# Last expert of a layer in pieces, 1/rms of the mixer applied at the evictions, and x moved in two parts

## The chip, the cores and the metric

One core of a Trainium2 chip runs the whole program. The metric is the device time of one execution in microseconds; lower is better. Engines: PE (TensorE), DVE (VectorE), ACT (ScalarE), POOL (GpSimd), and SP (SyncE), which here issues every DMA.

## What is computed

Two layers on x, 256 tokens by 1,024 features, float32. In each layer:

```python
u = rms_norm(x, norm_mix_g[l]) @ w_in[l]          # 1024 -> 3328 columns
aq, ak, av, bq, bf, bi, bg, cb, cc, cx = split(u)
o_a = differential_attention(aq, ak, av, ...)     # 4 heads, RMS norm of q and k
o_b = hgrn2(bq, bf, bi, bg, ...)                  # gated recurrence, chunks of 64
h = cc * cx; y = conv_w[0] * shift2(h) + conv_w[1] * shift1(h) + conv_w[2] * h
o_c = cb * y
x = x + concat(o_a, o_b, o_c) @ w_out[l]
h = rms_norm(x, norm_ffn_g[l])
# top-1 of 4 groups, top-2 of its 8 experts; expert = (silu(h Wg) * (h Wu)) Wd, 1024 -> 512 -> 1024
x = x + sum over the two chosen experts of gate * expert(h)
```

`rms_norm` divides each row (token) by the root of its mean square plus 1e-6 and multiplies by a gain per feature. The division commutes with the projection: it can be applied to the rows of u.

## The kernel before, in words

Tokens lie in two tiles of 128 rows (`TI` = 2). Five engine programs run side by side and meet at semaphores; each engine's order is written out by hand. A `Signal` counts, and `after(l, n)` is the value that its n-th event of layer l reaches.

**Start of a layer (mixer_norm, L1213).** ACT squares the rows of x and sums them (L899), DVE makes 1/rms by three Newton steps (`rsqrt`, L1182 to L1200), scales x by it into `h` (`normed`, L1204), PE transposes 128x128 blocks of `h` (L579), and DVE evicts them times the gain into `hT` (`take_transposed`, L1210). In layer 0 DVE first makes the rotary angles from the positions (`rotations`, L1095), and x arrives in one DMA (L371).

**Mixer.** PE multiplies `hT` with the sections of w_in as they land in the ring: `project_columns` (L649) gives features on partitions (HGRN's q and forget gate, and the three convolution parts), `project_rows` (L642) gives tokens on partitions. Thirteen results are evicted by ACT (`copy_out`, L901 to L905). The HGRN levels and the attention run between the projections. POOL does the output gate and the convolution (L491 to L512): gate + 1 (L499), gate product (L502), `ccT * cxT` (L504); then ACT multiplies by the taps (L1019), and POOL adds the two shifted parts (L508) and multiplies by `cbT` (L510), which signals `conv_ok`. PE waits for that (L811) before the first part of the output projection (L712), after transposing the attention output that DVE finishes (L791, L1401). After the taps, ACT has the squares for HGRN's norm (L1023).

**Experts.** 32 experts, 8 turns (`GROUPS`) of 4 units (`UG`), one expert each with 32 slots (`CAP`). A turn gathers its tokens by a one-hot product (L588), and transposes the gate matrix (L593). Each unit has "up" (L605: gate and up matrices side by side, moving width 256, four column groups of 32), silu and product and a 32x32 block transpose (L1155 to L1163), and "down" (L620), whose four 32-row results are copied to rows 32i to 32i+31 of `ye` by ACT (L890) and DVE (L1168). At the end of the turn four matmuls with 512 columns scatter all four units back to tokens (L628), and four DVE adds put them on x (L1173). A unit's three matrices are 2 MB each and live in a ring; SP issues gate and up of unit i when up of unit i-2 is done, and down when down of unit i-2 is done (L407 to L414), so two units are in flight:

```python
e.wait_ge(S.gu_ps.sem, S.gu_ps.after(turn, i - 1))
part(full, sg, ex, 0)
part(full, su, ex, 1)
e.wait_ge(S.ye_ps.sem, S.ye_ps.after(turn, i - 1))
part(full, sd, ex, 2)
```

(the semaphore starts at 2, so this waits for unit i-2). At the end of a layer the next layer's first sections of w_in queue behind the last unit's matrices (L417 to L429). At the end of the program SP stores x in one DMA (L485).

## Time and profile before

| | |
|---|---|
| median of 3 runs | 1287.55 us (1287.08 to 1288.71) |
| the profiled execution, its own time | 1283.46 us |
| its span, first to last instruction | 1281.7 us |
| mean granted TensorE clock | 0.864 |
| PE busy | 892.9 us (70%) |
| DVE busy | 522.3 us (41%) |
| ACT, POOL busy | 166.4 us, 25.9 us |
| moved by DMA | 442.05 MB, 345 GB/s over the span |

Layer 0's mixer runs to about 180 us, its experts to 642, layer 1's mixer to about 815, and its experts to the end. Busy shares are averages over stages with different limits, so each stage is to be read by itself. A float32 matmul stands in the profile as two records, a transpose as one. A granted clock of 1.00 is 2.4 GHz, 0.50 is 1.2 GHz.

### The profile page before, as it was taken

The numbers are of one execution on the slowest core, as the hardware profiler recorded it, in microseconds if no ns is written. First come the engines' busy times: TensorE is split into PE (matmuls) and PEld (weight loads), VectorE is DVE, ScalarE is ACT, GpSimd is POOL, SyncE is SP. The second block draws the span as 40 slices with busy tenths as digits, with TensorE's granted clock in tenths as the row PEclk, the third lists the DMA queues.
The fourth block names the chain that finished last, engine by engine and source line by source line (L and its number), as shares of the span: only waits on it lengthen the run. The fifth ranks groups of instructions, "written<-read, shape, count | busy, mean of one in ns | idle before, by whom it ended". The sixth has DMA issues, their size and how long they took to land.

```text
span 1281.7 us, 19451 instructions
## 1 busy us (share of the span) xinstructions
PE 892.9 (70%) x8069; PEld 531.1 (41%) x8069; DVE 522.3 (41%) x1309; ACT 166.4 (13%) x480; POOL 25.9 (2%) x63
## 2 busy tenths in 40 slices
PE   5999775766666566746679989757666575657665
PEld 4558453434334233424254574534333242324242
DVE  6666462423323232323257563624333232413232
ACT  2324110100000000000013241000000000000000
POOL 2001100000000000000000020000000000000000
PEclk9999877978888887888779999778788787978788
DMA  7824548799999999999984253498999999999995
GB/s 257 330 99 167 227 164 358 320 428 429 428 429 428 428 428 429 428 428 424 411 291 165 84 202 146 177 393 356 429 427 429 428 430 428 427 429 430 427 423 233
DMA packets 53986, 442.05 MB, mean 345 GB/s; under 512 B 9120, under 2 KB 12208, under 8 KB 29104
## 3 DMA queue, kind: packets, MB, share of 16 engines
q1 hardware_dynamic: 53936, 441.36, 83.3%
q8 instruction: 34, 0.56, 0.2%
...
## 4 chain that ended last, share of the span: by engine, by line
PE 54%; DMA 27%; DVE 14%; issue 3%; ACT 2%; SPq 0%; DVEq 0%; ACTq 0%
DMA ring<-in_expert_w_up 27%; PE bank L605 16%; PE bank L645 9%; PE bank L620 6%; PE bank L588 5%; PE bank L654 5%; PE bank L628 5%; PE bank L712 4%; DVE work L1157 2%; DVE work L1168 1%; PE bank L676 1%; DVE work L1163 1%; PE bank L579 1%; DVE work L1159 1%; DVE work L1161 1%
## 5 line engine op out<-in xcount | busy, mean ns | idle before, releaser
L605 PE MATMUL bank<-ring,work 128*32 128x256 f32 x4096 | 280.7, 435 | 118.6 <-DMA ring<-in_expert_w_up 118.2
L620 PE MATMUL bank<-ring,work 128*32 128x256 f32 x1856 | 154.7, 490 | 153.1 <-DVE work L1163 153.1
L605 PEld LDWEIGHTS bank<-ring,work 128*32 128x32 f32 x4096 | 153.2, 125 | 245.3 <-issue 158.7
L620 PEld LDWEIGHTS bank<-ring,work 128*32 128x32 f32 x1856 | 68.0, 135 | 231.0 <-DVE work L1163 180.1
L1155 DVE TENSOR_SCALAR work<-work 128x128 f32<-128x128 f32 x64 | 14.5, 227 | 359.0 <-ACT work L886 359.0
L1168 DVE COPY work<-bank 32x256 f32<-32x256 f32 x128 | 54.3, 424 | 162.9 <-PE bank L620 161.9
L645 PE MATMUL bank<-ring,hT 128*128 128x512 f32 x256 | 112.4, 593 | 0.0
L588 PE MATMUL bank<-work,h 128*128 128x128 f32 x512 | 78.4, 325 | 41.5 <-DVE work L1135 36.5
L588 PEld LDWEIGHTS bank<-work,h 128*128 128x128 f32 x512 | 75.4, 238 | 53.3 <-DVE work L1135 47.6
L890 ACT ACTIVATE work<-bank 32x256 f32<-32x256 f32 x128 | 47.8, 374 | 304.1 <-PE bank L620 303.3
L654 PE MATMUL bank<-hT,ring 128*128 128x256 f32 x320 | 75.5, 398 | 0.8 <-DVE hT L1210 0.8
L628 PE MATMUL bank<-work 128*128 128x512 f32 x128 | 58.7, 602 | 17.3 <-DVE work L1168 17.3
L645 PEld LDWEIGHTS bank<-ring,hT 128*128 128x128 f32 x256 | 47.7, 190 | 54.9 <-issue 54.5
L654 PEld LDWEIGHTS bank<-hT,ring 128*128 128x128 f32 x320 | 63.5, 201 | 10.7 <-DVE hT L1210 1.2
L886 ACT ACTIVATE work<-bank 128x128 f32<-128x128 f32 x64 | 17.8, 278 | 353.9 <-PE bank L605 353.9
L1157 DVE RECIPROCAL work<-work 128x128 f32<-128x128 f32 x64 | 61.0, 953 | 2.2
L712 PE MATMUL bank<-ring,hT 128*128 128x512 f32 x128 | 58.2, 611 | 2.8 <-ACT hT L1035 2.8
L1173 DVE TENSOR_TENSOR x<-bank,x 128x512 f32<-128x512 f32 x64 | 44.3, 692 | 28.5 <-PE bank L628 28.5
L628 PEld LDWEIGHTS bank<-work 128*128 128x128 f32 x128 | 23.0, 189 | 48.5 <-issue 48.5
L1148 DVE TENSOR_TENSOR work<-bank,gffn 128x512 f32<-128x512 f32 x32 | 21.9, 691 | 45.9 <-PE bank L588 45.9
L712 PEld LDWEIGHTS bank<-ring,hT 128*128 128x128 f32 x128 | 24.9, 198 | 32.1 <-issue 32.1
L905 ACT ACTIVATE work<-bank 128x512 f32<-128x512 f32 x26 | 15.5, 596 | 123.5 <-PE bank L645 71.5
(256 smaller groups left out, 655.0 us busy)
## 6 DMA issues: line engine op xcount, KB each, us to landing
...
maps<-in_expert_w_down SPq DMA_DIRECT2D x2, 2048.0 KB, 12.7
...
ring<-in_w_in SPq DMA_DIRECT2D x2, 1024.0 KB, 5.4
```

Of the source, the lines that this page charges most:

```text
L588: last = T.matmul(bank[half][:, k * P:k * P + P], h[:, i, 4 * half + k, :], sel[:, i, :], start=(i == 0), stop=(i == TI - 1))
L605: last = T.matmul(bank[GU_BANK[i % 2]][CAP * j:CAP * j + CAP, 0:2 * P], xg[:, k, CAP * i:CAP * i + CAP], gate_up[:, :, k, P * j:P * j + P] ...
L620: last = T.matmul(bank[5][CAP * q:CAP * q + CAP, 0:2 * P], actT[i % 2][:, CAP * j:CAP * j + CAP], down[j][:, 2 * P * q:2 * P * q + 2 * P], ...
L628: T.matmul(bank[(6, 7, 0, 1)[n]][:, :], gatT[:, i * P:i * P + P], ye[:, half * 512:half * 512 + 512], start=True, stop=True).then_inc(S.sc ...
L645: last = T.matmul(bank[b][:, :], hT[:, k, i * P:i * P + P], W[:, k, :], start=(k == 0), stop=(k == KT - 1))
L654: last = T.matmul(bank[b][:, c * SEQ:c * SEQ + SEQ], W[:, k, c0:c0 + P], hT[:, k, :], start=(k == 0), stop=(k == KT - 1))
L712: last = T.matmul(bank[2 * i + half][:, :], mixT[:, k, i * P:i * P + P], W[:, k, :], start=(k == 6), stop=(k == 3))
L890: last = A(ye[CAP * i:CAP * i + CAP, 2 * P * q:2 * P * q + 2 * P], bank[5][CAP * q:CAP * q + CAP, 0:2 * P], ACT.Copy)
L1148: TT(xg[:, 4 * half:4 * half + 4, :], bank[half][:, :].rearrange("p (k c) -> p k c", k=4), gffn[:, l, 4 * half:4 * half + 4].unsqueeze(2). ...
L1157: V.reciprocal(r, r).then_inc(c.step(), 1)
L1168: last = V.tensor_copy(ye[CAP * i:CAP * i + CAP, 2 * P * q:2 * P * q + 2 * P], bank[5][CAP * q:CAP * q + CAP, 0:2 * P])
L1173: TT(xs, bank[(6, 7, 0, 1)[n]][:, :], xs, ALU.add).then_inc(S.x_added.sem, 1)
```

## The change

- x is loaded in two DMAs, one for each 128 tokens, ahead of the gains and the positions, and stored in two.
- PE transposes x itself; 1/rms is made beside the projections. It is applied at the evictions: as ACT's scale where tokens are on partitions; for columns, PE spreads it over a row (`ones` times a diagonal, two matmuls of width 128), ACT copies that row, DVE multiplies HGRN's two parts by it while evicting (`take_columns`), and POOL multiplies `cbT` once and `ccT` twice.
- The last turn of a layer takes its last unit in pieces: gate alone, then the scatter of the first three units (96 rows), then up in two halves of 1 MB, then down in two halves. The four 32-row results stay on their partitions (one ACT and one DVE copy of 64x256), and eight matmuls of 32 rows by 256 columns scatter them into 8 banks, with the gate matrix of the last unit repeated four times (`spread`). DVE adds each tile of 128 tokens in one operation, and the next layer (or the store) starts on each tile by itself.

The core of the diff (`+` and `-` as usual):

```diff
+        rstd_row = sb("rstd_row", [P, SEQ])
+        diag = hg[:, Q_, 0:TI * P].rearrange("p (i t) -> p i t", i=TI)
...
+            rows_of = [a["x"][0][i * P:i * P + P] for i in range(TI)]
+            e.dma_start(x[:, 0, :], rows_of[0]).then_inc(x_in[0].sem, 16)
+            e.dma_start(x[:, 1, :], rows_of[1]).then_inc(x_in[1].sem, 16)
+            e.dma_start(gmix[:, :, :], by_feature("norm_mix_g")).then_inc(gain_in.sem, 16)
             e.dma_start(pos_i[:, :], a["positions"][0].rearrange("(i p) -> p i", p=P),
                         allow_slow_non_contiguous=True).then_inc(pos_in.sem, 16)
-            e.dma_start(gmix[:, :, :], by_feature("norm_mix_g")).then_inc(gain_in.sem, 16)
-            e.dma_start(x[:, :, :], a["x"][0].rearrange("(i p) d -> p i d", p=P)).then_inc(x_in.sem, 16)
             mixer_section(0, 0)
...
+                last = l * GROUPS + GROUPS - 1
+                for i in range(UG - 1):
+                    unit(ring_full, main, last, i, (GROUPS - 1) * UG + i)
+                sg, su, sd = slots_of(UG - 1)
+                e.wait_ge(main.gu_ps.sem, main.gu_ps.after(last, UG - 2))
+                part(ring_full, sg, NE - 1, 0)
+                w_up = a["expert_w_up"][l:l + 1, NE - 1:NE].rearrange("l e (p k) n -> p (l e k n)", k=KT)
+                for half in range(2):
+                    c = slice(half * SLOT // 2, half * SLOT // 2 + SLOT // 2)
+                    e.dma_start(slot(su)[:, c], w_up[:, c]).then_inc(up_half[half].sem, 16)
+                e.wait_ge(main.ye_ps.sem, main.ye_ps.after(last, UG - 2))
+                w_down = a["expert_w_down"][l:l + 1, NE - 1:NE].rearrange("l e (p j) n -> p (l e j n)", p=P)
+                for half in range(2):
+                    c = slice(half * SLOT // 2, half * SLOT // 2 + SLOT // 2)
+                    e.dma_start(slot(sd)[:, c], w_down[:, c]).then_inc(down_half[half].sem, 16)
+            for i in range(TI):
+                stream_ready(e, DEPTH, i)
+                e.dma_start(out[0][i * P:i * P + P], x[:, i, :]).then_inc(out_done.sem, 16)
+            e.wait_ge(out_done.sem, 16 * TI)
...
+                e.wait_ge(row_sb.sem, row_sb.after(l, 1))
                 settle(e)
                 G.tensor_scalar(egate, egate, 1.0, None, ALU.add).then_inc(gate_sum.sem, 1)
...
+                by_token = rstd_row[:, :].unsqueeze(1).to_broadcast([P, 2, SEQ])
+                for n, t in enumerate((cbT, ccT)):
+                    v = t.rearrange("p (c t) -> p c t", c=2)
+                    e.wait_ge(proj_sb.sem, proj_sb.after(l, 9 + n))
+                    G.tensor_tensor(v, v, by_token, ALU.mult).then_inc(conv_scaled.sem, 1)
+                e.wait_ge(conv_scaled.sem, conv_scaled.after(l, 2))
+                v = ccT.rearrange("p (c t) -> p c t", c=2)
+                G.tensor_tensor(v, v, by_token, ALU.mult).then_inc(conv_scaled.sem, 1)
+                e.wait_ge(proj_sb.sem, proj_sb.after(l, 11))
+                e.wait_ge(conv_scaled.sem, conv_scaled.after(l, 3))
                 G.tensor_tensor(ccT, ccT, cxT, ALU.mult).then_inc(conv_in.sem, 1)
                 e.wait_ge(taps_ok.sem, taps_ok.after(l, 1))
...
+            def last_experts(l, turn, loaded):
+
+                S = main
+                gathered(S, turn, True)
+                expert_units(S, turn, IN_TURN[0:2 * (UG - 1)], slots_of, loaded)
+                i = UG - 1
+                sg, su, sd = slots_of(i)
+                W = [slot(n).rearrange("p (k n) -> p k n", k=KT) for n in (sg, su)]
+
+                def half_up(part, ks):
+
+                    for k in ks:
+                        for j in range(4):
+                            last = T.matmul(bank[LAST_GU[part]][CAP * j:CAP * j + CAP, 0:P],
+                                            xg[:, k, CAP * i:CAP * i + CAP], W[part][:, k, P * j:P * j + P],
+                                            start=(k == 0), stop=(k == KT - 1))
+                    return last
+
+                e.wait_ge(ring_full[sg].sem, loaded(sg, i))
+                half_up(0, range(KT)).then_inc(gate_ps.sem, 1)
+
+                e.wait_ge(S.gat_sb.sem, S.gat_sb.after(turn, 1))
+                e.wait_ge(S.ye_act.sem, S.ye_act.after(turn, UG - 1))
+                e.wait_ge(S.ye_dve.sem, S.ye_dve.after(turn, UG - 1))
+                early = CAP * (UG - 1)
+                for n in range(4):
+                    T.matmul(bank[n][:, :], gatT[0:early, n // 2 * P:n // 2 * P + P], ye[0:early, n % 2 * 512:n % 2 * 512 + 512],
+                             start=True, stop=True).then_inc(S.scat_ps.sem, 1)
+
+                e.wait_ge(up_half[0].sem, up_half[0].after(l, 16))
+                half_up(1, range(0, 4))
+                e.wait_ge(up_half[1].sem, up_half[1].after(l, 16))
+                half_up(1, range(4, KT)).then_inc(S.gu_ps.sem, 1)
+                e.wait_ge(S.act_ok.sem, S.act_ok.after(turn, UG))
+                down = down_tiles(sd)
+                for j in range(4):
+                    if j % 2 == 0:
+                        e.wait_ge(down_half[j // 2].sem, down_half[j // 2].after(l, 16))
+                    for q in range(4):
+                        last = T.matmul(bank[5][CAP * q:CAP * q + CAP, 0:2 * P], actT[i % 2][:, CAP * j:CAP * j + CAP],
+                                        down[j][:, 2 * P * q:2 * P * q + 2 * P], start=(j == 0), stop=(j == 3))
+                last.then_inc(S.ye_ps.sem, 1)
+
+                e.wait_ge(S.x_added.sem, S.x_added.after(turn, 4))
+                e.wait_ge(S.ye_act.sem, S.ye_act.after(turn, UG))
+                e.wait_ge(S.ye_dve.sem, S.ye_dve.after(turn, UG))
+                for t in range(TI):
+                    for q in range(4):
+                        rows = slice(CAP * q, CAP * q + CAP)
+                        last = T.matmul(bank[4 * t + q][:, 0:2 * P], spreadT[rows, t * P:t * P + P], ye_last[rows, :],
+                                        start=True, stop=True)
+                    last.then_inc(tail_ps.sem, 1)
...
-                    e.wait_ge(h_ok.sem, h_ok.after(l, i + 1))
-                    transposed_rows(i, h[:, i, :, :])
+                    stream_ready(e, l, i)
+                    transposed_rows(i, x[:, i, :].rearrange("p (c k) -> p k c", k=KT))
...
                 W = section(0)
                 project_columns(W, 4, 0)
+                e.wait_ge(rstd_ok.sem, rstd_ok.after(l, 1))
+                for i in range(TI):
+                    last = T.matmul(bank[3][:, i * P:i * P + P], ones[:, :], diag[:, i, :], start=True, stop=True)
+                last.then_inc(row_ps.sem, 1)
                 project_columns(W, 5, 1)
...
-                    A(u[:, n - 1, :], bank[b][:, :], ACT.Copy).then_inc(proj_sb.sem, 1)
+                    if n <= 10:
+                        A(u[:, n - 1, :], bank[b][:, :], ACT.Copy, scale=rstd[:, (n - 1) % TI:(n - 1) % TI + 1]).then_inc(proj_sb.sem, 1)
+                    else:
+                        A(u[:, n - 1, :], bank[b][:, :], ACT.Copy).then_inc(proj_sb.sem, 1)
...
+                e.wait_ge(row_ps.sem, row_ps.after(l, 1))
+                A(rstd_row[:, :], bank[3][:, 0:SEQ], ACT.Copy).then_inc(row_sb.sem, 1)
+                e.wait_ge(cols_sb.sem, cols_sb.after(l, 1))
                 A(hg[:, Z0_, :], bq, ACT.Exp, scale=-1.0).then_inc(hg_act.sem, 1)
-                copy_out(2)
...
+            def last_experts(l, turn):
+                S, i, c = main, UG - 1, Chain(last_dve, l)
+                e.wait_ge(main.dve.sem, main.dve.after(l * (GROUPS - 1) + GROUPS - 2, DVE_G))
+                gathered(S, turn, codes, l, c, None, True)
+                expert_units(S, turn, IN_TURN[0:2 * (UG - 1)], c)
+                (gate, up), r = (bank[b][:, 0:P] for b in LAST_GU), silr[i % 2]
+                e.wait_ge(S.gu_exp.sem, S.gu_exp.after(turn, UG))
+                TS(r, sil[i % 2], 1.0, None, ALU.add).then_inc(c.step(), 1)
+                e.wait_ge(c.sem, c.last())
+                V.reciprocal(r, r).then_inc(c.step(), 1)
+                e.wait_ge(c.sem, c.last())
+                TT(r, gate, r, ALU.mult).then_inc(c.step(), 1)
+                for n in range(4):
+                    e.wait_ge(S.scat_ps.sem, S.scat_ps.after(turn, n + 1))
+                    xs = x[:, n // 2, n % 2 * 512:n % 2 * 512 + 512]
+                    TT(xs, bank[n][:, :], xs, ALU.add).then_inc(S.x_added.sem, 1)
+                e.wait_ge(S.gu_ps.sem, S.gu_ps.after(turn, UG))
+                e.wait_ge(c.sem, c.last())
+                TT(actv[i % 2], up, r, ALU.mult).then_inc(c.step(), 1)
+                e.wait_ge(c.sem, c.last())
+                V.transpose(actT[i % 2].rearrange("p (j c) -> p j c", j=4),
+                            actv[i % 2].rearrange("p (r j) -> p j r", j=4)).then_inc(S.act_ok.sem, 1)
+                e.wait_ge(S.ye_ps.sem, S.ye_ps.after(turn, UG))
+                V.tensor_copy(ye_last[P // 2:P, :], bank[5][P // 2:P, 0:2 * P]).then_inc(S.ye_dve.sem, 1)
+                e.wait_ge(S.x_added.sem, S.x_added.after(turn, 4))
+                for t in range(TI):
+                    e.wait_ge(tail_ps.sem, tail_ps.after(l, t + 1))
+                    xs = x[:, t, :].rearrange("p (q n) -> p q n", q=4)
+                    TT(xs, psum[:, 4 * t:4 * t + 4, 0:2 * P], xs, ALU.add).then_inc(tail_added.sem, 1)
+                c.end()
+
...
+                if spread_too:
+                    TT(gat, gat, gtmp, ALU.add).then_inc(c.step(), 1)
+                    e.wait_ge(c.sem, c.last())
+                    for i in range(TI):
+                        last = V.tensor_copy(spread[:, i, :].rearrange("p (q s) -> p q s", q=4),
+                                             gat[:, i, CAP * (UG - 1):CAP * UG].unsqueeze(1).to_broadcast([P, 4, CAP]))
+                        last.then_inc(S.gat_ok.sem if i else c.step(), 1)
...
                 def mixer_norm():
-                    e.wait_ge(sums_ok.sem, sums_ok.after(l, 2))
-                    rsqrt(rstd, ssq, D)
-                    for i in range(TI):
-                        normed(i).then_inc(h_ok.sem, 1)
                     if l == 0:
                         e.wait_ge(gain_in.sem, 16)
                     for n in range(4):
                         take_transposed(n, gmix)
+                    e.wait_ge(sums_ok.sem, sums_ok.after(l, 2))
+                    rsqrt(rstd, ssq, D)
+                    for i in range(TI):
+                        last = TS(diag[:, i, :], ident[:, :], rstd[:, i:i + 1], None, ALU.mult)
+                        last.then_inc(rstd_ok.sem if i else c.step(), 1)
                     V.memset(sT, 0.0).then_inc(c.step(), 1)
+
+                def take_columns(n, dst):
+
+                    e.wait_ge(proj_ps.sem, proj_ps.after(l, n))
+                    TT(dst.rearrange("p (c t) -> p c t", c=2), bank[3 + n][:, :].rearrange("p (c t) -> p c t", c=2),
+                       rstd_row[:, :].unsqueeze(1).to_broadcast([P, 2, SEQ]), ALU.mult).then_inc(cols_sb.sem, 1)
...
```

## Rows read from the trace of the kernel before

**Rows 1.** The page: GB/s moved, in 40 equal slices of the span.
```profile
GB/s 257 330 99 167 227 164 358 320 428 429 428 429 428 428 428 429 428 428 424 411 291 165 84 202 146 177 393 356 429 427 429 428 430 428 427 429 430 427 423 233
```

**Rows 2.** Chain of waits in order of time: start, us, what.
```profile
114.44 2.02 PE bank L703 x16
...
626.79 5.38 PE bank L605 x64
...
634.86 1.98 PE bank L620 x32
...
637.87 3.69 PE bank L628 x8
...
641.58 0.70 DVE x L1173
...
652.56 16.52 PE bank L654 x64
```

**Rows 3.** Instructions in order of time, layer 1's last turn: start, us, engine, line.
```profile
1232.88 0.33 SPq L397 DMA_DIRECT2D ring<-in_expert_w_gate  x1
...
1247.22 5.73 PE L605 MATMUL bank<-ring,work 128*32 128x256 f32 x64 [0.78 <-DMA ring<-in_expert_w_up]
...
1255.67 1.45 PEld L620 LDWEIGHTS bank<-ring,work 128*32 128x32 f32 x32 [3.21 <-DVE work L1163]
1255.68 1.93 PE L620 MATMUL bank<-ring,work 128*32 128x256 f32 x32 [2.73 <-DVE work L1163]
...
1261.90 5.22 PE L605 MATMUL bank<-ring,work 128*32 128x256 f32 x64 [4.29 <-DMA ring<-in_expert_w_up]
...
1277.30 0.40 SPq L485 DMA_DIRECT2D out<-x  x1
```

**Rows 4.** The same view, start of the program.
```profile
1.78 0.47 SPq L371 DMA_DIRECT2D x<-in_x  x1
...
3.00 1.27 DVE L1100 CAST small<-pos_i 128x2 f32<-128x2 int32 x1 [3.00 <-DMA pos_i<-in_positions]
...
12.19 2.21 DVE L1204 TENSOR_SCALAR h<-x,small 128x1024 f32<-128x1024 f32 x2
...
18.12 16.31 PE L654 MATMUL bank<-hT,ring 128*128 128x256 f32 x64
```

**Rows 5.** PE by stretches: us, PE busy (records), granted clock, DMA share, GB/s.
```profile
616.20:626.70 10.50, 2.78 (x36) 0.68 1.00 424
...
652.50:656.00 3.50, 3.44 (x8) 0.50 1.04 385
...
1247.00:1253.00 6.00, 5.73 (x64) 0.63 0.99 421
```

**Rows 6.** Groups by line and form: count, busy us, mean ns, idle before.
```profile
L1163 DVE STREAM_TRANSPOSE work<-work 128x128 f32<-128x128 f32 x64 | 25.8, 404 | 2.2
...
L1346 DVE TENSOR_TENSOR work<-work,small 128x1024 f32<-128x1024 f32 x4 | 4.9, 1226 | 0.1
```

**Rows 7.** DMA issues: count, KB each, median us to landing.
```profile
x<-in_x SPq DMA_DIRECT2D x1, 1024.0 KB, 5.3
out<-x SPq DMA_DIRECT2D x1, 1024.0 KB, 4.0
```

**Rows 8.** Instructions in order of time, end of layer 0's mixer: POOL, DVE, PE.
```profile
124.66 1.26 POOL L504 TENSOR_TENSOR work<-work 128x512 f32<-128x512 f32 x1
124.76 3.31 DVE L1386 TENSOR_TENSOR maps<-maps,small 128x2048 f32<-128x2048 f32 x1
...
128.54 3.16 POOL L508 TENSOR_TENSOR work<-work 128x510 f32<-128x510 f32 x2 [2.62 <-ACT work L1019]
...
129.33 1.24 DVE L1185 TENSOR_SCALAR small<-small 128x4 f32<-128x4 f32 x1
...
131.78 1.27 POOL L510 TENSOR_TENSOR hT<-work 128x512 f32<-128x512 f32 x1
...
136.87 4.52 PE L712 MATMUL bank<-ring,hT 128*128 128x512 f32 x8
```

132 lines of the change are left out of this document (82 added, 50 removed).

## Prediction

> **What bounds the kernel now.** I read the page's strips first: in both expert stages the DMA moves 428 to 430 GB/s in nearly every slice, slice after slice, and falls away in the two mixer stages [rows 1]. So the expert stages run at the pace of the weights, and the mixers at that of the engines. A change to either end of an expert stage therefore shifts all that follows; one inside it is hidden. The chain of waits in order of time gives the seam between the layers [rows 2]: the last up matrix lands at 626.79, and from there to 652.56, where the mixer's first projection starts, it is a pure chain of short steps, 25.8 us. The instructions in order of time give the same tail at the end of the program [rows 3]: up lands at 1261.90, the store is issued at 1277.30 and takes 4.0 us [rows 7], so 19.4 us. The last down matrix is behind up in one stream. At 429 GB/s 2 MB take 4.9 us, so gate has landed 4.9 us before up (622 and 1257), the first half of up 2.4 us before, and down 4.9 us after it (631.7, 1266.8). These are the places that the change touches, with the start of the program and the mixer's evictions.
>
> **The sum, part by part** (negative is a gain), in the profiled execution's times.
>
> Start of the program. The DVE begins its rotations at 3.00, when the positions land, and has them and the rsqrt done for the scaling at 12.19; the projection starts at 18.12 [rows 4]. Of this the change removes rsqrt, scaling and the transposes' wait for them from the path. It also puts both parts of x ahead of the positions on SP. The whole x lands 5.3 us after its issue at 1.78 [rows 4, 7]; issued some 1 us earlier, with positions behind it, the positions land at 6.0 to 6.3 instead of 3.0. Rotations took 6.3 us (3.00 to 9.3), partly beside POOL's set-up; I take 5.5. Then four takes at 0.7 us: 6.1 + 5.5 + 2.8 = 14.5, so **-3.5**. Bounds: positions at 4.3 give -4.5, rotations at full 6.3 us and positions at 7 give -2.0.
>
> Tail of each layer. New order on PE: gate alone after down of unit 2; scatter of the first 96 slots; two halves of up; down; the row-tiled scatter. Gate or up alone is 64 records of width 128. The full 64 records of width 256 take 3.6 to 5.4 us; the trace has no narrow ones. Below: half the stream, 1.8 us. Above: no gain, 3.6 us. Weight loads of 32 columns have been issued at 1.45 us for 32, 45 ns each [rows 3], which gives 2.9 us; it is the nearest row and I take it. The new scatter is the old one, 3.67 us, but earlier.
> - End of the program: down of unit 2 ends at 1257.6 [rows 3], gate to 1260.6, scatter to 1264.3, up to 1267.2 (both halves are there), multiply and transpose 0.75 (0.40 of it the transpose [rows 6]), down 1.98 to 1269.95 (landed at 1266.8 latest), the copies 0.55 (one of 64x256 each instead of two of 32x256), so 1270.5. A group of four 32-row matmuls: the nearest row is the scores' (L703), 64 rows high, eight matmuls of width 256 (16 records) in 2.02 us [rows 2], so 1.0 for four; bounds 0.45 and 1.7. Then two adds of 1,024 columns, 1.23 us each by the row of that width [rows 6]: 1271.5, 1272.75, 1274.0. Half the store: 4.0 us [rows 7] less 1.2 us of bytes at 429 GB/s = 2.8. End at 1276.9 instead of 1281.3: **-4.4**. Bounds -6.8 (narrow at 1.8 us; then down's landing is the limit) and -0.7 (narrow at 3.6 us and row tiles serial).
> - Seam: the granted clock was 0.68 between 616.2 and 626.7 [rows 5], so gate from 622.0 is half at the low level: 4.4 us, to 626.4; scatter to 630.1, up to 633.0, down from 633.75 to 635.7, copies to 636.3, matmuls 1.0, adds to 638.55 and 639.8. The old last add ended at 642.3. Then transposes of x directly (the first half beside the second add), and four takes on DVE, 0.69 us each, from 639.85: projection at 642.7 instead of 652.56, **-9.9**. The squares, rsqrt and the two diagonals (2.3 + 2.3 + 0.3 us) run beside the first 8 us of projection. Bounds: -13.7 and -6.8.
>
> For the row tiles I used 1.0 us for a group of four. The Trainium skill, TensorEngine Tiling (Array Packing), section Tiling Modes, has four tiles of 32 rows that work independently, which would be one stream, 0.45 us by this trace's rate; the sum would be 0.5 us lower per layer, and no row here shows such tiles.
>
> More issues on SP (one more for up, one for down, one for the store and for x, at 0.33 to 0.47 us each) stand behind nothing: SP's queue is ahead of the stream. The last group's two extra copies on DVE and two transposes on PE (up to 0.4 us) delay the issue for unit 2, but the stream still has some 3 us in hand there (unit 2's gate and up, issued from 1232.88, have landed at 1247.22 [rows 3], 14.3 us for 9.8 us of bytes and some 1 to 2 us of latency): 0, bound +0.8 in all. If that cover is gone, all of it counts.
>
> Mixer, PE: two matmuls of width 128 for the row of 1/rms, 0.45 us each layer on the path since PE is busy throughout the projections: **+0.9**. Evictions: the scale rides on copies that exist. Two move from ACT (0.60) to DVE (0.69) and wait for the row's copy, 1 us later for the HGRN chain, which ran over 5 us ahead of PE's need: 0.
>
> Mixer, POOL: three new products of 128x512 stand between the gate product and the old conv product, ahead of the taps (ACT) and ahead of the three last POOL steps, on which PE's first part of the output projection waits. One takes 1.26 us [rows 8]. The rows show more: POOL and DVE shut each other out. DVE's 2,048-wide product takes 3.31 us where two of 1,024 make 2.45, and starts beside a POOL product; the first POOL add waits for the DVE product (3.16 us for two that need 2.2); and DVE steps of 4 elements take 1.24 us while POOL adds [rows 8]. So I lay both queues out in turn: products at 124.7, 128.1, 130.5, 131.9 with DVE's two between them; taps (2.6 us) 133.2 to 135.8; POOL's last three until 140.2 instead of 133.05. PE had been ready for it at 136.87, so the cover of 3.8 us is overrun by **3.3** per layer, **+6.6**. ACT's taps stand ahead of the squares for the HGRN norm, whose result comes at 143.7, before PE's 144.5: no further loss. Bounds per layer: 0 (only 3.8 us of products, exactly the cover) and +5.5 (PE falls to the low clock in the longer gap).
>
> Sum: -3.5 - 9.9 - 4.4 + 0.9 + 6.6 = **-10.3** against the profiled execution (1283.46; span 1281.7), 1273.2. The median of the runs is 1287.55, 4.1 above it; I take the difference over: 1277.3.
>
> **Rivals.**
> 1. The POOL products are hidden. For: the cover of 3.8 us equals three products. Against: the mutual exclusion just read [rows 8]. Then -16.9: 1270.7. Chance 0.18.
> 2. PE stays at the high clock over the seam. The projection of layer 1 begins at 0.50 [rows 5] after some 6 us without PE work but transposes; the new gaps are under 2 us. Against: the unit that started at 1247.22 after gaps of that kind ran at 0.63 [rows 3, 5]. Then -2.7 more: 1274.6. Chance 0.12.
> 3. Narrow matmuls cost as much as full ones and the row tiles run one after another: the seam gains only 6.8 and the end only 0.7: -3.5 - 6.8 - 0.7 + 7.5 = -3.5, 1284.0. Chance 0.12, half of it within the bound of no change.
> 4. Slower: the POOL products are the mechanism. They sit ahead of the taps in POOL's queue; gains without them are 16.9 us, so from 8.5 us of delay per layer the change loses, that is when the three take (8.5 + 3.8)/3 = 4.1 us each, against 1.26 to 2.0 seen. At 5.5 us each the delay is 12.7 per layer: -16.9 + 25.4 = +8.5, 1296. Chance 0.04.
> 5. It does less than it says: the halves of up and down land no earlier than the whole (the sixteen engines skewed). PE is behind the stream there, so it costs under 1 us; inside the forecast.
>
> **How the numbers follow.** Forecast and its near misses 0.54, rivals 0.18, 0.12, 0.12, 0.04. A measurement of this kernel tells 0.2% (2.6 us) from no change. Faster: 0.54 + 0.18 + 0.12 + 0.06, less 0.04 for several upper bounds together = 0.86; within 0.2%: 0.10; slower 0.04. The range reaches from rival 1 with a part of the seam's bound (1268) to rival 3 (1284).
>
> **What the profile after would show.** Projection in layer 0 from about 14.5; first projection of layer 1 10 us after the last up half, with the same low clock at its start; POOL products of 1.26 to 2 us in line behind the gate product and PE's first output projection waiting on the last of them, not on DVE; a store of 2.8 us. I am wrong if the narrow records are not near 45 ns, if that wait ends elsewhere, or if the expert stages, which I left as they are, get longer or shorter.

## The result, and the profile after

The changed kernel takes 1274.78 us (median of 9 runs, 1270.47 to 1280.96) where the kernel before, run beside it, takes 1288.71 (9 runs, 1281.24 to 1296.96): a ratio of 0.9881, 95% interval 0.9846 to 0.9917. The forecast was 1277.3. The profiled execution of the changed kernel took 1270.47 us with a span of 1268.7, that of before 1283.46 and 1281.7, so the sum stands beside a difference of 13.0 us. Both profiled executions lie 4 to 5 us below their medians, the changed kernel's is the lowest of its nine, so the two differences, 13.0 and 13.9, agree.

The page after: the strips of GB/s and of the granted clock.
```profile
PEclk9999788879888888888899989778888888879789
GB/s 258 355 84 194 200 166 320 291 428 429 429 429 428 428 428 428 429 429 424 420 389 195 100 245 87 184 390 330 429 428 428 428 429 429 429 428 428 428 423 316
```
The two plateaus at some 428 GB/s stand as in [rows 1], but the slices just ahead of the first one changed: 320 and 291 where there were 358 and 320. The first two turns of the expert stage are not yet at the pace of the weights.

The start of the program after (start us, us, engine, line).
```profile
2.15 0.47 SPq L389 DMA_DIRECT2D pos_i<-in_positions  x1
...
5.04 3.65 PE L622 MATMUL psum<-ident,x 128*128 128x128 f32 x16 [5.04 <-POOL masks L594]
...
6.96 0.21 DVE L1229 CAST small<-pos_i 128x2 f32<-128x2 int32 x1 [6.96 <-DMA pos_i<-in_positions]
...
12.01 2.48 DVE L1384 TENSOR_TENSOR hT<-psum,gmix 128x512 f32<-128x512 f32 x4
...
14.75 1.65 PE L761 MATMUL psum<-hT,ring 128*128 128x256 f32 x3
```
Against [rows 4] the scaling of h is gone and the transposes run at 5.04 beside the rest; the positions now land at 6.96, and VectorE's rotations and takes behind them set the start, 14.75 for 18.12.

The seam between the layers after, PE and what it waits for, in order of time.
```profile
625.21 1.92 PE L655 MATMUL psum<-ring,work 128*32 128x128 f32 x64
...
627.06 3.70 PE L668 MATMUL psum<-work 96*128 96x512 f32 x8
...
630.69 1.95 PE L655 MATMUL psum<-ring,work 128*32 128x128 f32 x64
...
633.50 1.07 PE L681 MATMUL psum<-ring,work 128*32 128x256 f32 x16 [0.85 <-DVE work L1286]
...
635.10 1.07 PE L681 MATMUL psum<-ring,work 128*32 128x256 f32 x16 [0.53 <-DMA ring<-in_expert_w_down]
...
636.81 1.15 PE L691 MATMUL psum<-work 32*128 32x256 f32 x16 [0.64 <-DVE work L1289]
637.65 2.35 DVE L1294 TENSOR_TENSOR x<-psum,x 128x1024 f32<-128x1024 f32 x2 [0.99 <-PE psum L691]
...
642.45 7.17 PE L761 MATMUL psum<-hT,ring 128*128 128x256 f32 x32 [1.23 <-DVE hT L1384]
```
From the last up matrix's matmuls to the projection it is 11.8 us (630.69 to 642.45) where [rows 2] have 25.8. Gate alone takes 1.92, the scatter of the first 96 slots stands ahead of up, up takes 1.95, and then PE waits for the second half of down: the stream, not PE, ends this chain. The projection's first 32 records take 7.17 us.

PE by stretches after: us, PE busy, PEld, DVE, ACT, POOL, granted clock, DMA share, GB/s.
```profile
642.45:651.45 9.00, 9.00 (x44) 7.99 (x45) 4.57 (x20) 0.59 (x2) 0.00 (x0) 1.00 1.05 386
```
Where [rows 5] have the low level (0.50, that is 1.2 GHz) the clock is now at its high level, 2.4 GHz, from the first column on.

The end of the program after, in order of time, and two rows of the DMA issues.
```profile
1255.62 1.95 PE L655 MATMUL psum<-ring,work 128*32 128x128 f32 x64
...
1260.56 1.07 PE L681 MATMUL psum<-ring,work 128*32 128x256 f32 x16 [1.06 <-DMA ring<-in_expert_w_down]
...
1262.27 1.15 PE L691 MATMUL psum<-work 32*128 32x256 f32 x16 [0.64 <-DVE work L1289]
...
1264.36 1.47 SPq L518 DMA_DIRECT2D out<-x  x2
```
```profile
x<-in_x SPq DMA_DIRECT2D x2, 512.0 KB, 4.5
out<-x SPq DMA_DIRECT2D x2, 512.0 KB, 2.7
```
13.1 us from up to the end of the span, 19.8 in [rows 3]; the half store lands in 2.7 us, the whole one took 4.0 [rows 7].

The end of layer 0's mixer after, POOL with DVE and ACT beside it.
```profile
119.66 1.27 POOL L536 TENSOR_TENSOR work<-work 128x512 f32<-128x512 f32 x1 [22.29 <-DVE work L1632]
...
120.89 4.54 POOL L541 TENSOR_TENSOR work<-work,rstd_row 128x512 f32<-128x512 f32 x2
120.99 3.31 DVE L1570 TENSOR_TENSOR maps<-maps,small 128x2048 f32<-128x2048 f32 x1
...
125.51 2.13 POOL L544 TENSOR_TENSOR work<-work,rstd_row 128x512 f32<-128x512 f32 x1
126.43 1.23 DVE L1359 TENSOR_SCALAR small<-small 128x4 f32<-128x4 f32 x1
...
127.79 1.27 POOL L547 TENSOR_TENSOR work<-work 128x512 f32<-128x512 f32 x1
...
129.10 2.50 ACT L1148 ACTIVATE work<-work,table 128x256 f32<-128x256 f32 x6 [6.87 <-POOL work L547]
...
131.67 2.75 POOL L551 TENSOR_TENSOR work<-work 128x510 f32<-128x510 f32 x2 [2.61 <-ACT work L1148]
```
Three new products (L541 twice, L544) take 6.7 us where three undisturbed ones would take 3.8, and all that follows on POOL stands behind them [rows 8]. PE's own rows show what the first output projection waits for:
```profile
135.93 5.91 PE L822 MATMUL psum<-ring,hT 128*128 128x512 f32 x8 [2.65 <-POOL hT L553]
```
L553 is POOL's last step. The eight records take 5.91 us where they took 4.52 [rows 8].

### The profile page after: what moved, and what is told of

Same layout as the page of the kernel before. It is cut to its first block, busy times and chain, and to the rows that moved or that the text cites. A ratio compares the mean times of both kernels' runs of the same rounds, so it can differ in the third digit from the quotient of the medians.

```text
span 1268.7 us, 19814 instructions
## 1 busy us (share of the span) xinstructions
PE 888.4 (70%) x8241; PEld 530.9 (42%) x8241; DVE 526.1 (41%) x1319; ACT 165.1 (13%) x476; POOL 38.5 (3%) x69
## 4 chain that ended last, share of the span: by engine, by line
PE 53%; DMA 28%; DVE 11%; issue 3%; POOL 2%; ACT 1%; SPq 1%; DVEq 0%; POOLq 0%
DMA ring<-in_expert_w_up 24%; PE psum L719 15%; PE psum L752 9%; PE psum L631 6%; PE psum L734 6%; PE psum L822 5%; PE psum L761 5%; PE psum L704 4%; DMA ring<-in_expert_w_down 3%; DVE work L1336 2%; PE psum L786 1%; DVE work L1342 1%; DVE work L1347 1%; DVE work L1338 1%; DVE work L1340 1%
## 5 line engine op out<-in xcount | busy, mean ns | idle before, releaser
L719 PE MATMUL psum<-ring,work 128*32 128x256 f32 x3968 | 270.4, 433 | 114.4 <-DMA ring<-in_expert_w_up 114.4
L734 PE MATMUL psum<-ring,work 128*32 128x256 f32 x1792 | 147.2, 485 | 147.6 <-DVE work L1342 147.6
L719 PEld LDWEIGHTS psum<-ring,work 128*32 128x32 f32 x3968 | 147.7, 125 | 236.0 <-issue 148.0
L734 PEld LDWEIGHTS psum<-ring,work 128*32 128x32 f32 x1792 | 64.6, 133 | 221.1 <-DVE work L1342 173.6
L1347 DVE COPY work<-psum 32x256 f32<-32x256 f32 x124 | 52.6, 424 | 155.2 <-PE psum L734 154.2
L752 PE MATMUL psum<-ring,hT 128*128 128x512 f32 x256 | 112.4, 593 | 0.0
L631 PE MATMUL psum<-work,h 128*128 128x128 f32 x512 | 79.6, 328 | 43.2 <-DVE work L1304 36.2
L631 PEld LDWEIGHTS psum<-work,h 128*128 128x128 f32 x512 | 76.3, 240 | 55.4 <-DVE work L1304 47.2
L761 PE MATMUL psum<-hT,ring 128*128 128x256 f32 x320 | 72.5, 385 | 1.2 <-DVE hT L1384 1.2
L752 PEld LDWEIGHTS psum<-ring,hT 128*128 128x128 f32 x256 | 47.7, 190 | 54.9 <-issue 54.5
L822 PE MATMUL psum<-ring,hT 128*128 128x512 f32 x128 | 60.0, 627 | 8.1 <-POOL hT L553 5.3
L761 PEld LDWEIGHTS psum<-hT,ring 128*128 128x128 f32 x320 | 61.0, 193 | 9.8 <-DVE hT L1384 1.4
L704 PE MATMUL psum<-work 128*128 128x512 f32 x112 | 51.4, 601 | 15.2 <-DVE work L1347 15.2
L822 PEld LDWEIGHTS psum<-ring,hT 128*128 128x128 f32 x128 | 25.3, 202 | 39.2 <-issue 39.2
## 6 DMA issues: line engine op xcount, KB each, us to landing
maps<-in_expert_w_down SPq DMA_DIRECT2D x2, 2048.0 KB, 12.2
```

Source lines behind the costliest of these rows:

```text
L631: last = T.matmul(bank[half][:, k * P:k * P + P], h[:, i, 4 * half + k, :], sel[:, i, :], start=(i == 0), stop=(i == TI - 1))
L704: T.matmul(bank[(6, 7, 0, 1)[n]][:, :], gatT[:, i * P:i * P + P], ye[:, half * 512:half * 512 + 512], start=True, stop=True).then_inc(S.sc ...
L719: last = T.matmul(bank[GU_BANK[i % 2]][CAP * j:CAP * j + CAP, 0:2 * P], xg[:, k, CAP * i:CAP * i + CAP], gate_up[:, :, k, P * j:P * j + P] ...
L734: last = T.matmul(bank[5][CAP * q:CAP * q + CAP, 0:2 * P], actT[i % 2][:, CAP * j:CAP * j + CAP], down[j][:, 2 * P * q:2 * P * q + 2 * P], ...
L752: last = T.matmul(bank[b][:, :], hT[:, k, i * P:i * P + P], W[:, k, :], start=(k == 0), stop=(k == KT - 1))
L761: last = T.matmul(bank[b][:, c * SEQ:c * SEQ + SEQ], W[:, k, c0:c0 + P], hT[:, k, :], start=(k == 0), stop=(k == KT - 1))
```

## The experiments

All of them are read by one division of the span, worked out from the starts of PE's rows in the profiled executions: start of the projection, of the scores' second group, of the first output projection, of the gather in the first and in the last turn of the expert stage. The columns are the us between them; "seam" reaches from the last turn's gather in layer 0 to the projection of layer 1, "end" from the last gather to the end. A gather is not tied to one place of the weight stream, so a few us can move between neighbouring columns of the expert stage; where that matters, the count below goes from a landing.

Ratios are to the kernel before, run beside each group. Its medians were 1294.96 us (e1 to e4), 1291.83 (e5 to e8) and 1288.78 (e9 to e11), with single runs from 1281 to 1297, so kernels of different groups are compared by stretches first.

| kernel | to proj. | to scores | to out | to gather 0 | 7 turns | seam | to scores | to out | to gather 0 | 7 turns | end | span |
|---|---|---|---|---|---|---|---|---|---|---|---|---|
| before | 18.12 | 96.32 | 22.43 | 49.29 | 401.90 | 64.50 | 96.53 | 22.43 | 49.40 | 402.62 | 58.16 | 1281.7 |
| changed | 14.75 | 95.91 | 25.27 | 50.67 | 404.22 | 51.63 | 94.54 | 25.27 | 49.83 | 402.07 | 54.54 | 1268.7 |
| e5 (again) | 14.76 | 96.32 | 25.27 | 50.89 | 403.64 | 52.27 | 94.54 | 25.28 | 49.91 | 402.09 | 54.63 | 1269.6 |
| e1 tail undone | 14.75 | 96.56 | 25.22 | 51.04 | 403.96 | 60.16 | 94.54 | 25.26 | 51.00 | 403.42 | 61.19 | 1287.1 |
| e2 norm undone | 21.56 | 94.09 | 22.44 | 49.44 | 401.97 | 59.21 | 95.82 | 22.44 | 50.73 | 402.97 | 55.73 | 1276.4 |
| e3 no products | 14.79 | 96.65 | 22.43 | 50.71 | 403.34 | 52.54 | 94.54 | 22.44 | 49.54 | 401.93 | 54.59 | 1263.5 |
| e4 POOL early | 14.76 | 96.72 | 22.43 | 50.74 | 403.55 | 52.39 | 94.53 | 22.43 | 49.54 | 402.40 | 54.71 | 1264.2 |
| e6 no row tiles | 14.78 | 97.27 | 25.22 | 51.40 | 404.42 | 55.69 | 94.54 | 25.22 | 51.49 | 404.56 | 56.01 | 1280.6 |
| e7 pieces only | 14.78 | 96.04 | 25.23 | 50.77 | 403.43 | 56.89 | 94.54 | 25.24 | 51.05 | 403.55 | 58.18 | 1279.7 |
| e8 positions early | 13.12 | 96.29 | 22.44 | 50.50 | 403.18 | 53.16 | 94.54 | 22.42 | 50.93 | 404.06 | 54.66 | 1265.3 |
| e9 four fills | 14.77 | 96.84 | 25.21 | 51.16 | 404.23 | 56.40 | 97.36 | 25.23 | 51.41 | 404.68 | 54.41 | 1281.7 |
| e10 six fills | 14.76 | 97.38 | 25.21 | 51.44 | 403.55 | 59.88 | 96.10 | 25.23 | 50.78 | 403.32 | 54.75 | 1282.4 |
| e11 one store | 14.75 | 96.04 | 25.27 | 50.72 | 403.96 | 52.40 | 94.53 | 25.22 | 51.33 | 403.77 | 55.21 | 1273.2 |

**e1: the tail undone.** The last expert is taken whole as before, the new norm and the parts of x stay.
```diff
-                last_experts(l, l * GROUPS + GROUPS - 1)
+                experts(main, l * GROUPS + GROUPS - 1, IN_TURN, codes, l, l * GROUPS + GROUPS - 1, None, (6, 7, 2, 3))
```


> The last turn of a layer is as before the change (whole matrices, one scatter at the end); the rest is the changed kernel, and each tile of 128 tokens still goes on by itself. My theory: the pieces, the early scatter and the row tiles took about 5.7 us out of the way from the last up matrix to the last add in layer 0 and 6.7 us at the end, so 10 to 12 us come back, near 1285 us by medians, and from up's landing to the last add it is 15.5 us again. Rival (the tail was hidden and the gain came from the norm and the clock): within 3 us of the changed kernel.

Measured 1288.92 (1286.55 to 1290.98), 0.997 of before, interval 0.9937 to 1.0003: no gain clear of the noise is left. Against e5 the seam is longer by 7.9 and the end by 6.6, 14.5 together; expected were 5.7 and 6.7. The seam is more than expected because the old chain ran at the low clock here: PE at the seam, in order of time, has
```profile
631.06 6.42 PE L707 MATMUL psum<-ring,work 128*32 128x256 f32 x64 [4.79 <-DMA ring<-in_expert_w_up]
640.21 3.54 PE L722 MATMUL psum<-ring,work 128*32 128x256 f32 x32 [2.73 <-DVE work L1330]
```
The same rows took 5.38 and 1.98 in [rows 2], 2.6 us less. The last 3 us of e1's 17.5 against e5 lie in stages that the edit doesn't touch.

**e2: the norm undone.** h is scaled ahead of the transposes as before, no row of 1/rms, no products; the tail and x in two parts stay.
```diff
+                    rsqrt(rstd, ssq, D)
+                    for i in range(TI):
+                        normed(i).then_inc(h_ok.sem, 1)
...
-                for i in range(TI):
-                    last = T.matmul(bank[3][:, i * P:i * P + P], ones[:, :], diag[:, i, :], start=True, stop=True)
-                last.then_inc(row_ps.sem, 1)
```


> The mixer scales x by 1/rms before the transposes again, and POOL's three products are gone; last turn, loads and stores as changed. My theory: start +6 us (the positions now land late and rsqrt and scaling follow them), seam +7.7 us and +2.5 us for a low clock at its projection, against -7.5 us for the products and -1.4 us for the row: about +7 us, 1282 us. Rival (the products were hidden): +14 us, 1289 us.

Measured 1277.61 (1276.65 to 1278.25), 0.9883 of before, interval 0.9818 to 0.9949: 2.8 us above the first median of the changed kernel and 5.8 above e5's, by spans 6.8 above e5; expected was +7. The norm gives 6.8 at the start (21.56 to 14.76) and 6.9 at the seam, takes 2.84 twice in the mixers, and the rest is in the stretches whose clock moves. Of the 6.8, 2 us are this execution's own: the positions landed at 8.90, with the same issues ahead of them, and at 6.96 in the changed kernel. The start of 21.56 is also later than before's 18.12, where they landed at 3.00: with x in front of the positions on SP, the old order of work pays for part of their late landing. The two seam terms don't add: tail alone -5.3, norm alone -4.3, both -12.2 against 64.50. The missing 2.6 are as much as e1's chain lost by the low clock just shown.

**e3: no products.** The three products on POOL are left out, so the convolution's inputs are not scaled by 1/rms.
```diff
-                by_token = rstd_row[:, :].unsqueeze(1).to_broadcast([P, 2, SEQ])
-                for n, t in enumerate((cbT, ccT)):
...
-                e.wait_ge(conv_scaled.sem, conv_scaled.after(l, 3))
```


> POOL's three products by the row of 1/rms are left out, so the convolution part is not scaled; all else as changed. My theory: PE's wait for the last POOL step before the output projection goes, 3.3 to 4.2 us per layer, 6.5 to 8.5 us in all, 1267 us. Rival (hidden): no change, 1275 us.

Measured 1266.76 (1263.16 to 1268.6), ratio 0.9801 (0.9733 to 0.9869). Scores to output projection is 22.43 in both layers, as before, instead of 25.27: the products cost 2.84 a layer there. What stays is the 1.4 us more than before from the output projection to layer 0's gather, so that part is not theirs.

**e4: the products early.** The three products stand ahead of the gate product in POOL's program; everything is computed.
```diff
-                e.wait_ge(gate_rec.sem, gate_rec.after(l, 1))
-                gview = egate.rearrange("p (i n) -> p i n", i=TI)
-                G.tensor_tensor(gview, gview, bib[:, :, HB * DB:2 * HB * DB], ALU.mult).then_inc(gate_ok.sem, 1)
                 by_token = rstd_row[:, :].unsqueeze(1).to_broadcast([P, 2, SEQ])
                 for n, t in enumerate((cbT, ccT)):
...
+                e.wait_ge(gate_rec.sem, gate_rec.after(l, 1))
+                gview = egate.rearrange("p (i n) -> p i n", i=TI)
```


> The same three products, but in POOL's order ahead of the gate product, where POOL idles for some 18 us waiting for DVE's reciprocal. My theory (their place costs, not their work): as without them, 6 to 8 us below the changed kernel, 1267.5 us, all of the computation done. Rival (POOL and DVE shut each other out, so the time only moves to DVE's softmax steps): 0 to -3 us, 1272 to 1275 us.

Measured 1266.23 (1264.08 to 1269.42), ratio 0.9801 (0.9734 to 0.9868). POOL in order of time:
```profile
103.71 1.28 POOL L538 TENSOR_TENSOR work<-work,rstd_row 128x512 f32<-128x512 f32 x1 [5.52 <-ACT work L1037]
111.51 1.27 POOL L538 TENSOR_TENSOR work<-work,rstd_row 128x512 f32<-128x512 f32 x1 [6.52 <-ACT work L1037]
112.85 1.27 POOL L541 TENSOR_TENSOR work<-work,rstd_row 128x512 f32<-128x512 f32 x1
```
Same work, 1.27 us each, done by 114.1 while POOL had nothing else. It costs nothing: 22.43 again. It was the place in the queue, not the work.

**e5: the changed kernel again**, beside e6 to e8, unchanged.

> The changed kernel unaltered, as the reference for the three beside it and for the spread: about 1275 us, profile stages within 1 us of the first profile except where the granted clock differs.

Measured 1271.83 (1271.26 to 1277.32), ratio 0.9862 (0.9819 to 0.9904).

**e6: no row tiles.** The last 32 slots are scattered by four matmuls of 32 rows by 512 columns (eight records), one after another, and added in four steps.
```diff
-                        last = T.matmul(bank[4 * t + q][:, 0:2 * P], spreadT[rows, t * P:t * P + P], ye_last[rows, :],
...
+                for n in range(4):
+                    T.matmul(bank[n][:, :], gatT[early:P, n // 2 * P:n // 2 * P + P], ye[early:P, n % 2 * 512:n % 2 * 512 + 512],
```


> The last unit's result goes to rows 96 to 127 of ye by four copies of 32x256 again and is scattered by four matmuls of 32 rows by 512 columns and four adds; pieces and early scatter stay. Theory: from down's end to the last add 5.5 us instead of 3.8, so 1.7 us per layer, 3.4 us in all, 1278 us. Rival (a group of row tiles runs one after another, so tiling gains nothing): 0 to +1 us.

**e7: the pieces alone.** As e6, and the scatter of all 128 slots comes at the end again; only the order gate, two halves of up, two halves of down is left.
```diff
-                    T.matmul(bank[n][:, :], gatT[0:early, n // 2 * P:n // 2 * P + P], ye[0:early, n % 2 * 512:n % 2 * 512 + 512],
...
+                    T.matmul(bank[n][:, :], gatT[:, n // 2 * P:n // 2 * P + P], ye[:, n % 2 * 512:n % 2 * 512 + 512],
```


> Gate, up and down in pieces, but no early scatter: one scatter of all 128 slots at the end, four copies, four adds. Theory now that narrow records take 30 ns: PE has time for the early scatter while it waits for the last half of down, so taking it away frees nothing and the end is as without row tiles, +3.4 us, 1278 us. Rival (my prediction's view, PE behind the stream in the tail): up ends 3.7 us earlier and down is done earlier, so 0 to -2 us per layer against the kernel without row tiles.

Measured 1283.19 for e6 (1282.18 to 1285.56; 0.9943, 0.9915 to 0.9972) and 1283.39 for e7 (1280.01 to 1284.34; 0.9937, 0.9913 to 0.996). Both are some 11 us above e5, and 5 above what was expected. In all three kernels PE waits, in both layers, for the landing of down's second half, so the count goes from there. To layer 1's projection it is 7.4 us in e5, 11.6 in e6 and 12.0 in e7; to the end of the span 8.1, 11.4 and 12.1. So e6 loses 7.5 us and e7 8.6, where 3.4 was expected of each. In e6 the seam's rows are
```profile
637.23 1.07 PE L681 MATMUL psum<-ring,work 128*32 128x256 f32 x16 [0.43 <-DMA ring<-in_expert_w_down]
...
639.38 5.01 PE L689 MATMUL psum<-work 32*128 32x512 f32 x8 [1.08 <-DVE work L1289]
644.32 3.67 PE L622 MATMUL psum<-ident,x 128*128 128x128 f32 x16
```
5.0 us for what takes 1.15 with row tiles, and 5.5 at the end; the granted clock was 0.50 from 641.7 to 648.3, and at the high level eight records of 512 columns take 3.7. That is some 3 of the 7.5. In e7 the second half of down is slower:
```profile
635.11 1.93 PE L676 MATMUL psum<-ring,work 128*32 128x256 f32 x16 [0.52 <-DMA ring<-in_expert_w_down]
```
1.93 for 1.07, and 1.94 at the end. Without the early scatter PE stood idle for 0.7, 1.3 and 1.5 us ahead of it, and the granted clock was 0.50 from 632.4 to 642.4. From the landing on, the early scatter is worth 0.5 and 0.7 us, and this row alone is 0.9. So it frees no time in the order of work, as was expected; what it is worth here goes with the clock. The other 3.5 us of e6 and 1.5 of e7 lie ahead of that landing, e6's in both layers, e7's in layer 1. The last three runs are about those.

**e8: positions first.** e4, and the positions' DMA is issued ahead of x.
```diff
+            e.dma_start(pos_i[:, :], a["positions"][0].rearrange("(i p) -> p i", p=P),
+                        allow_slow_non_contiguous=True).then_inc(pos_in.sem, 16)
             e.dma_start(x[:, 0, :], rows_of[0]).then_inc(x_in[0].sem, 16)
...
-            e.dma_start(pos_i[:, :], a["positions"][0].rearrange("(i p) -> p i", p=P),
-                        allow_slow_non_contiguous=True).then_inc(pos_in.sem, 16)
```


> Products ahead of the gate product, and the positions' DMA issued ahead of x. Theory: the rotations run from 3.0 to 9.3 us again while x lands and is transposed, the four takes follow, and the projection starts at 12.2 to 12.6 us instead of 14.8: 2.3 us below the kernel with early products, 1264 us. Rival (the first section of w_in lands last): no change, 1266 us.

Measured 1265.0 (1262.12 to 1269.72; 0.9794, 0.9748 to 0.984), which e4's runs can't be told from. The start gains 1.6 us where 2.3 was expected, and something else is late next: PE's rows have
```profile
12.94 0.26 PE L830 MATMUL psum<-ident,prow 16*128 16x16 f32 x1 [4.03 <-DMA prow<-in_conv_w]
13.12 1.22 PE L761 MATMUL psum<-hT,ring 128*128 128x256 f32 x2
```
The takes were done at 11.8, but the transpose of the parameter rows stands ahead of the projection on PE and waits for conv_w.

**e9, e10: idle time at the seam.** Four and six fills of the state tile on VectorE ahead of layer 1's first take.
```diff
+                    if l == 1:
+                        for q in range(4):
+                            V.memset(sT, 0.0).then_inc(delay.sem, 1)
+                            e.wait_ge(delay.sem, q + 1)
```


> The changed kernel with four more fills of the 128x1024 state tile on VectorE (0.91 us each in its profile, about 3.9 us together) ahead of layer 1's first take; nothing else differs, and it is computed in full. It tests where the 6 us came from that the kernel without row tiles lost outside the tail. Theory A (the granted clock's level falls otherwise on turns that begin later): the projection of layer 1 starts near 646.3 instead of 642.45 and the scores near 741, and then the stretch from the output projection to the first gather takes more than the 49.8 us of the changed kernel (50.7 to 51.5, as in the two kernels whose scores began at 741.7 and 743.3), and first gather to last gather more than 402.1 (403 to 405): the total is 3.9 plus 1.5 to 4, some 1276 to 1279 us where the changed kernel has 1271 to 1272. Theory B (the stages last as long as before, and the loss had to do with that edit itself): 49.8 and 402.1 stay, and the total is up by 3.9 alone, 1275 to 1276.

> As the one before, with six fills (about 5.8 us): the projection of layer 1 starts near 648.3, where the kernel without row tiles had it at 648.78. Theory A (the clock's level depends on when the turns begin): output projection to first gather near 51.5, first to last gather near 404.6, so 4 us on top of the delay, 1280 to 1282 us. Theory B (the edit itself): 49.8 and 402.1 stay, total up by 5.8, 1277 to 1278.

**e11: one store.**
```diff
-                e.dma_start(out[0][i * P:i * P + P], x[:, i, :]).then_inc(out_done.sem, 16)
+            e.dma_start(out[0].rearrange("(i p) d -> p i d", p=P), x[:, :, :]).then_inc(out_done.sem, 16)
```


> The changed kernel with one store of the 1 MB output after the second add, as before the change; all else as changed. From the rows the store of one piece takes 4.0 us from issue to landing and that of half 2.7, and the second half is issued 1.1 us after the first. Theory: the two halves save 4.0 - 2.7 = 1.3 us at the end, less what the first half still moves, so this kernel ends 0.9 to 1.3 us later (span 1270 instead of 1268.7 to 1269.6), within 0.1 per cent of the changed kernel. Rival: both halves share the same 16 queues and the split saves nothing: 0 to 0.3 us later.

Measured: e9 1282.16 (1281.37 to 1284.43; 0.9941, 0.9913 to 0.997), e10 1283.08 (1280.47 to 1284.91; 0.9961, 0.993 to 0.9991), e11 1275.0 (1271.61 to 1278.83; 0.9899, 0.9856 to 0.9943).

Each fill takes 1.19 us with its wait, so four put in 4.8 and six 7.1 us, not the 3.9 and 5.8 that were expected. The span of e9 is 12.1 longer than that of e5, that of e10 12.8. The projection behind the fills is back at the low clock: PE's rows in e9 are
```profile
648.61 9.99 PE L762 MATMUL psum<-hT,ring 128*128 128x256 f32 x32 [4.82 <-DVE hT L1385]
...
658.88 7.07 PE L762 MATMUL psum<-hT,ring 128*128 128x256 f32 x32
```
9.99 where the changed kernel has 7.17: after 4.8 us of idle PE the projection began at the low level. That is 2.8 of the 12.1. PE by stretches, in e9 and then in e10:
```profile
647.60:654.20 6.60, 5.59 (x13) 4.51 (x14) 4.89 (x21) 0.00 (x0) 0.00 (x0) 0.50 1.05 387
```
```profile
648.70:655.30 6.60, 3.08 (x7) 2.52 (x8) 5.99 (x20) 0.00 (x0) 0.00 (x0) 0.50 1.05 387
```
The low stretch is as long in both, but e10's projection starts only at 652.22 and has 3.2 us of it, where e9's starts at 648.61 and has 5.7. So six fills lose 1.6 us at the projection and four 2.8, and delays don't add one to one.

With the fills, e9 is accounted for by 7.6 us and e10 by 8.7. Another 1.3 us of e9 lie in layer 0, ahead of the fills, and 4.1 in routing and the turns of layer 1, 51.41 and 404.68 for 49.91 and 402.09. Those two figures are what theory A had foreseen.

But e11 has them without a delay. Up to its last two instructions it is the changed kernel, and its routing and turns in layer 1 took 51.33 and 403.77. By stretches, the changed kernel's routing and first turn, and then e11's:
```profile
762.26:812.09 49.83, 39.94 (x147) 23.11 (x147) 23.28 (x99) 5.28 (x19) 0.00 (x0) 0.88 0.39 152
812.09:864.18 52.09, 33.52 (x427) 22.52 (x427) 22.60 (x64) 4.48 (x13) 0.00 (x0) 0.83 0.76 312
```
```profile
762.89:814.22 51.33, 41.44 (x147) 23.61 (x147) 23.43 (x100) 5.28 (x19) 0.00 (x0) 0.87 0.38 149
814.22:867.40 53.18, 34.62 (x427) 21.76 (x427) 22.62 (x64) 4.48 (x13) 0.00 (x0) 0.79 0.75 305
```
The same 147 and 427 records keep PE busy 1.50 and 1.10 us longer, and the stretches are longer by 1.50 and 1.09, at granted clocks of 0.87 and 0.79 for 0.88 and 0.83. The same program spends different shares of these stages at the low level from one execution to the next, 3.2 us in layer 1 here. So the 3.5 and 1.5 us of e6 and e7 can be the chance of one profile, and theory A is not shown. The medians point the same way. The changed kernel has 1271.8 and 1274.8, and e11 without its 1.2 us for the store 1273.8. With the 7.5 to 8.7 us found in place, e6, e7, e9 and e10 should come out at 1279 to 1284, and they took 1282.2 to 1283.4. So no more than some 4 us, and perhaps nothing, came from stages that answer elsewhere.

For the store, both kernels are read from the start of the row-tiled scatter to the end of the span: 6.4 us in the changed kernel (1262.27 to 1268.7), 7.6 in e11 (1265.61 to 1273.2). Two halves save 1.2 us; expected was 0.9 to 1.3. The medians can't show it.

## Why the prediction was right, point by point

The time, the sign and the range held, and the places were right; several sizes were off, in both directions. In the profiled executions, by the rows of PE named above (predicted, then measured):

| term | predicted | measured |
|---|---|---|
| start of the projection, layer 0 | -3.5 | -3.4 |
| projections, row of 1/rms and clock, layer 0 | +0.45 | -0.4 |
| mixer 0 to the first gather | +3.3 | +4.2 |
| expert stage 0, first gather to the last up's matmuls | 0 | +3.5 |
| seam, the last up's matmuls to the projection | -9.9 | -14.0 |
| projections, layer 1 | +0.45 | -2.0 |
| mixer 1 to the first gather | +3.3 | +3.3 |
| expert stage 1 | 0 | +2.5 |
| end, the last up's matmuls to the end | -4.4 | -6.7 |
| sum | -10.3 | -13.0 |

**Start: right.** The projection was expected at 14.5 and starts at 14.75. Positions landed at 6.96 and not at 6.0 to 6.3, the takes took 2.48 and not 2.8. e8 shows that the positions' landing was the wait, up to the next one 1.6 us earlier.

**The tail: right mechanism, two terms too dear.** "45 ns each" for a narrow record was mis-sized: 64 of them take 1.92 to 1.95 us, 30 ns each. The row taken was the issue time of 32-column weight loads among matmuls twice as wide; the lower bound, half of the full stream, was the nearer. A group of four row-tiled matmuls was put at 1.0; 16 records take 1.15, about 0.5 to 0.6 for a group. With both PE is done so early that it waits 0.53 and 1.06 us for down's second half, which is the case that the prediction had given as the bound: 13.7 at the seam and 6.8 at the end. Measured 14.0 and 6.7. Of these 0.5 and 0.7 us are that up now starts behind the scatter, after its landing; they come back in the expert stages. Counted from up's landing it is 13.5 and 6.1.

The Trainium skill, TensorEngine Tiling (Array Packing), section Tiling Modes, has four tiles of 32 rows work independently; 1.15 us for 16 records agrees with that and not with one after another: full-width records of 256 columns take 0.22 us each in the projection (32 in 7.17), 16 of them 3.6. The prediction had weighed it and stayed with the dearer row.

**The clock at the seam: rival 2 was true**, though the prediction gave it 0.12. The projection of layer 1 ran at 1.00 from the first column, 7.17 us for 32 records, as the second 32 (7.07). It had been priced at -2.7; the layer 1 row above, +0.45 for the two extra matmuls and -2.0 in all, gives -2.45. Its argument against, that a unit after gaps of that kind ran at 0.63, did not hold here: PE's gaps over the seam are now 0.5 to 1.2 us, where before had one of 5 us ahead of up and one of 6.6 ahead of the transposes, and e9, with 4.8 us, has the low level back. e1 and e2 tell the two gaps apart. e1 has the old tail, with 4.8 us idle ahead of up, and the new norm: its projection ran high, 94.54 to the scores as in the changed kernel. e2 has the new tail and the old norm, with 6.8 us idle ahead of the transposes: 95.82, at 0.50 from 648.71 to 652.2. So the level was won by the norm and not by the tail. What else is needed stays open: short gaps alone don't keep the level up. e7 had none over 1.5 us and ran at 0.50 from 632.4 to 642.4, e6 from 641.7 to 648.3, e11 from 639.1 to 642.4, and the projection that follows had the high level in all three (94.54 to the scores).

**The products: right, and rival 1 wrong.** The wait was where it was said to be, on POOL's last step and not on DVE. The products took 4.54 for two and 2.13 for the third, with DVE's product of 2,048 columns in their middle and its four-element steps at 1.23 beside the third, so mutual exclusion set their time; 2.84 us of the 3.3 is theirs (e3 and e4), in each layer. The other 1.4 in layer 0 stay in e3 and e4, which have no products on the path, so it isn't the longer gap of the upper bound. It is the clock even so: the row L822 above took 5.91 for 4.52. By stretches, before and then the changed kernel:
```profile
136.87:138.60 1.73, 1.73 (x4) 0.70 (x4) 1.50 (x7) 0.60 (x1) 0.00 (x0) 0.50 1.06 455
```
```profile
135.93:140.40 4.47, 4.47 (x6) 1.89 (x7) 3.15 (x10) 0.00 (x0) 0.00 (x0) 0.50 0.17 73
```
A low stretch that began before the output projection reaches 1.8 us into the output projection in before and 4.6 in the changed kernel; in e4 it is 4.8, and in layer 1 2.9 in the changed kernel and 5.9 in e11. From there to the gather these take 49.3, 50.7, 50.7, 49.8 and 51.3 us, within 0.1 us of 48.4 plus half of that time. So this column is settled by how far the low stretch reaches into it. What sets that is not shown. e4 shows that rival 1's time was to be had: 1266.2 with the three products moved in one program, and the prediction had looked only at whether they are hidden where they are.

The Trainium skill, GPSIMD Engine Reference, section Key points, says that the engine shares its SBUF interfaces with VectorE and contends with DVE instructions of two SBUF inputs; the trace agrees for the 2,048-wide product (3.31 us, beside 4.54 for two POOL products that take 2.54 alone).

**The expert stages: the step that failed.** "The expert stages, which I left as they are" were 3.5 and 2.5 us longer. Where the stream is full they can't be: from the landing of the third turn's first up matrix to that of the eighth turn's it is 293.6 to 293.8 us in both layers of every kernel. What moves is what stands ahead of the full stream and behind it. From the first gather to the landing of the third turn's first up matrix, where PE sets the pace, it is 2.3 us more in layer 0 and 2.1 in layer 1; in the last turn up landed 0.6 us later in layer 0 and 0.2 earlier in layer 1; and 0.5 and 0.7 are the last up's wait behind the scatter.

The first of these is the largest, and its cause was not found. It took 102.7 and 102.3 us in before and 104.0 to 105.5 in all other profiles, also in e2 (104.0 and 105.1), which has the old norm, and in e1 (105.4 and 105.3), which has the old tail. So no one part of the change brings it all back. What all twelve share, such as x in two parts, was not tested, and chance has a share: in layer 1 the same program came out 1.1 us apart here, 104.4 in the changed kernel and 105.5 in e11.

So the total was right in part because errors cancelled: -4.1 and -2.3 in the tails and -3.3 in the projections against +0.9 and +6.0 elsewhere. That rival 2's own number, 1274.6, was hit to 0.2 us is luck of the same kind.

**The best version** is e4, or e8, which adds the positions' order: 1266.2 and 1265.0, 0.98 and 0.979 of before, both below both kernels.
